# Trunk kernel: the conv mixer's weights in place from the first full period on, with four u buffers and five v buffers

## The reference, cut to what matters

```
a = rms_norm(x); z = a @ w_in                       # rwkv | conv | gates
o_r = rwkv7(z_rwkv) @ rwkv_w_o                      # 512 x 1024 weights ("w_r")
o_c = conformer_conv(z_conv) @ conv_w_o             # 512 x 1024 weights ("w_c")
h = x + (g_r * o_r + g_c * o_c) @ w_out
c = rms_norm(h)
# PEER: 8 heads x 16 = 128 experts per token, of 16384
idx, gates = top_k_product_keys(c @ w_q)
coef = gates * gelu(<c, u_tab[idx]>)                # one row of 4 KB per token and expert
h = h + sum_e coef_e * v_tab[idx_e]                 # another row of 4 KB
h = h + sigmoid(rms_norm(h) @ w_gate) * (p @ w_proj)
out = rms_norm(h)
```

## Time and profile before

| what | value |
|---|---|
| median of 3 runs | 3468.84 us (3466.03 to 3469.73) |
| the profiled execution | 3462.86 us, span 3461.2 us |
| DVE / PE / POOL busy | 69% / 78% / 57% of the span |
| data moved | 1253.76 MB, of it 1073.87 MB by the gathers (queue q0) |
| mean rate | 362 GB/s; 394 to 410 in the page's slices 11 to 35, which the full periods fill |

### The profile page before, as it was taken

How to read it: one execution, slowest core, us unless ns; L and a number is a source line. 1 busy time by engine, 2 the same in 40 slices (tenths; PEclk the granted TensorE clock), 3 DMA queues, 4 the chain that set the end, 5 groups by cost and what they waited for, 6 DMA issues and landing times.

```text
span 3461.2 us, 41395 instructions
## 1 busy us (share of the span) xinstructions
PE 2703.1 (78%) x15236; PEld 1218.4 (35%) x15236; DVE 2383.9 (69%) x6070; ACT 526.2 (15%) x1165; POOL 1970.5 (57%) x2093
## 2 busy tenths in 40 slices
PE   9987988898866777677677777786777678778887
PEld 7764655565423322332232323331333112111111
DVE  5549889988898779877987798779875677520000
ACT  3213212221211011101110021101110121110001
POOL 0003334333577676767676767666766667757663
PEclk9999999999889887988798968886888779789999
DMA  6547899889999999999999999999999999999995
GB/s 209 182 147 264 297 337 337 288 288 332 343 395 406 402 404 408 408 401 400 409 409 399 399 409 409 399 394 409 408 403 401 410 410 408 410 378 390 397 378 215
DMA packets 381194, 1253.76 MB, mean 362 GB/s; under 512 B 40384, under 2 KB 76480, under 8 KB 380224
## 3 DMA queue, kind: packets, MB, share of 16 engines
q0 software_dynamic: 294912, 1073.87, 79.9%
q1 hardware_dynamic: 83776, 176.20, 14.2%
q10 hardware_dynamic: 2304, 1.05, 0.1%
HBM read 1221.47 MB, written 29.49 MB: 361 GB/s over the span
## 4 chain that ended last, share of the span: by engine, by line
DMA 34%; PE 17%; POOL 14%; DVE 10%; issue 7%; ACT 0%; SPq 0%; POOLq 0%; ACTq 0%; DVEq 0%
DMA e_u<-in_u_tab,e_idx 14%; DMA e_v<-in_v_tab,e_idxT 10%; POOL e_v L780 7%; DMA e_a_rstd<-in_u_tab,e_idx 7%; PE e_acc L1087 5%; POOL e_u L763 5%; DVE e_u L1933 3%; PE e_acc L1157 3%; PE e_pd L985 3%; PE e_pd L1056 2%; POOL e_a_rstd L763 1%; DMA e_u<-in_v_tab,e_idxT 1%; DVE e_a_rstd L1933 1%; DMA e_x<-h_after_experts 1%; DVE e_gbc L1662 1%
## 5 line engine op out<-in xcount | busy, mean ns | idle before, releaser
L1087 PE MATMUL e_acc<-e_v,e_wd 128*32 128x512 f32 x3636 | 1112.8, 725 | 494.8 <-DMA e_v<-in_v_tab,e_idxT 480.2
L763 POOL DMA_INDIRECT e_u<-in_u_tab,e_idx x820 | 792.6, 967 | 903.0 <-DVE e_dots L1933 516.7
L1933 DVE CUSTOM_DVE_ANT_0 e_u<-e_u,e_c 128x1024 f32<-128x1024 f32 x820 | 996.2, 1215 | 378.9 <-DMA e_u<-in_u_tab,e_idx 373.4
L780 POOL DMA_INDIRECT e_v<-in_v_tab,e_idxT x909 | 863.6, 950 | 332.3 <-issue 218.6
L1087 PEld LDWEIGHTS e_acc<-e_v,e_wd 128*32 128x32 f32 x3636 | 147.7, 116 | 1141.3 <-DMA e_v<-in_v_tab,e_idxT 931.0
L1157 PE MATMUL e_acc<-e_v 128*128 128x384 f32 x1216 | 429.7, 499 | 11.6 <-ACT e_wd L1368 11.6
L1933 DVE CUSTOM_DVE_ANT_0 e_a_rstd<-e_a_rstd,e_c 128x1024 f32<-128x1024 f32 x204 | 247.8, 1215 | 94.7 <-DMA e_a_rstd<-in_u_tab,e_idx 94.1
L1662 DVE SCALAR_TENSOR_TENSOR e_gbc<-e_hc,e_cw,e_gbc 128x128 f32<-128x128 f32 x960 | 309.3, 343 | 1.2
L1157 PEld LDWEIGHTS e_acc<-e_v 128*128 128x128 f32 x1216 | 225.2, 193 | 160.4 <-issue 33.6
L763 POOL DMA_INDIRECT e_a_rstd<-in_u_tab,e_idx x204 | 196.6, 964 | 146.6 <-DVE e_dots L1933 115.4
L1942 DVE TENSOR_TENSOR e_hh<-e_hh,e_acc 64x512 f32<-64x512 f32 (+1 forms) x24 | 16.4, 682 | 249.6 <-PE e_acc L1087 249.1
(11 more groups left out here) (268 smaller groups left out, 2681.0 us busy)
## 6 DMA issues: line engine op xcount, KB each, us to landing
e_v<-in_w_in SPq DMA_DIRECT2D x76, 512.0 KB, 6.1
e_u<-in_w_in SPq DMA_DIRECT2D x38, 512.0 KB, 3.8
e_v<-in_v_tab,e_idxT POOLq DMA_INDIRECT x909
e_u<-in_u_tab,e_idx POOLq DMA_INDIRECT x820
e_ring<-in_w_c SPq DMA_DIRECT2D x32, 256.0 KB, 11.5
e_zb<-in_w_c SPq DMA_DIRECT2D x32, 256.0 KB, 8.4
e_ring<-in_w_r SPq DMA_DIRECT2D x32, 256.0 KB, 6.4
e_zb<-in_w_r SPq DMA_DIRECT2D x32, 256.0 KB, 9.0
```

Source lines behind the costliest of these rows:

```text
L763: pool.indirect_dma_start(out=u[m % UR][:, :], out_offset=None, in_=io["u_tab"], in_offset=bass.IndirectOffsetOnAxis(ap=idx[n % 2][:, j:j ...
L780: pool.indirect_dma_start(out=v[i], out_offset=None, in_=io["v_tab"], in_offset=bass.IndirectOffsetOnAxis(ap=idxT[n % (LAG + 1)][:, k:k + ...
L1087: last = pe.matmul(acc[rows, cols], w[:, at_:at_ + 32], v[v_place(m)[0]][:, cols], start=(step == 0), stop=True, skip_group_check=True)
L1933: dve.tensor_tensor_reduce(u[m % UR][:, :], u[m % UR][:, :], c[:, :], 1.0, 0.0, ALU.mult, ALU.add, dots[n % 2][:, j:j + 1]).then_inc(s_dot, 1)
```

## The change

From the front of tile 3 on, which runs in period 2 (`RESIDENT_FROM = 3`), the eight `w_c` blocks lie in eight fixed places and are not loaded again: the four `e_ring` buffers, the two halves of the sixth v buffer and the two halves of `e_a_rstd`. They are loaded once, in period 2. From period 2 on the u side therefore has four buffers (`u_place`, `u_user`; five in periods 0 and 1) and the v side five. The `w_r` blocks go through six places in `e_zb` (`stream_load`): blocks 0 to 5 when the recurrence is done, blocks 6 and 7 after the y products 0 and 1 have freed the first two places. In periods 8 and 9, where the mixer no longer runs, v again has eleven buffers.

```diff
-UR, UW, VR, RING, RINGS = 5, 4, 6, 4, 8
+UR, UW, VR, VW, RING, RINGS = 4, 4, 5, 6, 4, 8
+U_EARLY, RESIDENT_FROM, W_R = UR + 1, 3, 6
+VL = VR + UR + 2
+def u_place(m):
+    early = (RESIDENT_FROM - 1) * NSEL
+    if m < early:
+        return m % U_EARLY, m // U_EARLY + 1
+    i, k = (m - early) % UR, (m - early) // UR + 1
+    return i, len(range(i, early, U_EARLY)) + k
+def u_user(m):
+    early = (RESIDENT_FROM - 1) * NSEL
+    if m < early:
+        return m - U_EARLY if m >= U_EARLY else None
+    i = (m - early) % UR
+    return m - UR if m - early >= UR else range(i, early, U_EARLY)[-1]
...
+        v = [v_all[:, i, :] for i in range(VR)] + [u[i][:, :] for i in range(UR)] + [v_all[:, VR, :], a_rstd[:, :]]
+        w_c = [r[:, :, :] for r in ring[0:RING]] + [x[:, i * PAIRS * P:(i + 1) * PAIRS * P].rearrange("p (i t) -> p i t", i=PAIRS)
+                                              for x in (v_all[:, VR, :], a_rstd) for i in range(2)]
...
+            def resident_load(m):
+                first = RESIDENT_FROM
+                if m < RING:
+                    sp.wait_ge(s_wu, 2 * KT * (first - 1) + RINGS + m + 1)
+                elif m < RING + 2:
+                    sp.wait_ge(s_bm, BLOCKS * COL_TILES)
+                else:
+                    sp.wait_ge(s_dot, (first - 1) * NSEL)
+                sp.dma_start(w_c[m], io["w_c"][m]).then_inc(s_ring[RESIDENT_AT], 16)
+
+            def stream_load(n, m):
+                if m < W_R:
+                    sp.wait_ge(s_rp, REC_PE * 2 * (n + 1))
+                else:
+                    sp.wait_ge(s_wu, 2 * KT * n + KT + m - W_R + 1)
+                i = stream_turn(n, m)[0]
+                sp.dma_start(w_r[m % W_R][:, :, :], io["w_r"][m]).then_inc(s_ring[i], 16)
...
-                for k in ring_loads_at(n, s):
-                    ring_load(n, k // KT, k % KT)
+                if n < RESIDENT_FROM:
+                    for k in ring_loads_at(n, s):
+                        ring_load(n, k // KT, k % KT)
+                else:
+                    if n == RESIDENT_FROM and 40 <= s < 40 + KT:
+                        resident_load(s - 40)
+                    for m in range(KT):
+                        if s == (MIX_AT + m if m < W_R else product_slot(KT + m - W_R)):
+                            stream_load(n, m)
...
-                if m >= UR:
-                    pool.wait_ge(s_dot, m - UR + 1)
+                if u_user(m) is not None:
+                    pool.wait_ge(s_dot, u_user(m) + 1)
```

More of the change, by code:

```diff
@@ L177, in v_user @@
         return m - VR if m >= VR else None
-    if m - alone >= VR + UR:
-        return m - VR - UR
+    if m - alone >= VL:
+        return m - VL
     return m - VR if m - alone < VR else None
@@ L331, in trunk @@
         flat_zb = zb[:, :, :, :, :, :].rearrange("p c w i a t -> p (c w i a t)")
-        ring += [flat_zb[:, i * PAIRS * P:(i + 1) * PAIRS * P].rearrange("p (i t) -> p i t", i=PAIRS) for i in range(RINGS - RING)]
+        w_r = [flat_zb[:, i * PAIRS * P:(i + 1) * PAIRS * P].rearrange("p (i t) -> p i t", i=PAIRS) for i in range(W_R)]
+        ring += w_r[0:RINGS - RING]
         arena = buf("e_arena", [P, 34 * P])
@@ L360, in trunk @@
         pt = gbc[:, 0, 0:PLE // P, :]
-        u = [*(buf(f"e_u{i}", [P, D]) for i in range(UW)), a_rstd]
-        v_all = buf("e_v", [P, VR, D])
-        v = [v_all[:, i, :] for i in range(VR)] + [u[i][:, :] for i in range(UR)]
+        u = [buf(f"e_u{i}", [P, D]) for i in range(UR)]
+        u_all = [*u, a_rstd]
+        v_all = buf("e_v", [P, VW, D])
+        v = [v_all[:, i, :] for i in range(VR)] + [u[i][:, :] for i in range(UR)] + [v_all[:, VR, :], a_rstd[:, :]]
+        w_c = [r[:, :, :] for r in ring[0:RING]] + [x[:, i * PAIRS * P:(i + 1) * PAIRS * P].rearrange("p (i t) -> p i t", i=PAIRS)
+                                              for x in (v_all[:, VR, :], a_rstd) for i in range(2)]
         wd = [buf(f"e_wd{i}", [P, QUARTER * WROW]) for i in range(2)]
@@ L371, in trunk @@
         w_a = [u[i][:, :].rearrange("p (k c) -> p k c", k=KT) for i in range(UW)]
-        w_b = [v[3 + i].rearrange("p (k c) -> p k c", k=KT) for i in range(BW)]
+        w_b = [v_all[:, 3 + i, :].rearrange("p (k c) -> p k c", k=KT) for i in range(BW)]
         taken = blocks_at + KT * BEHIND_T
@@ L458, in trunk @@
         s_c = sem("e_tile_switched")
-        s_u = [sem(f"e_u_in{i}") for i in range(UR)]
-        s_v = [sem(f"e_v_in{i}") for i in range(VR + UR)]
+        s_u = [sem(f"e_u_in{i}") for i in range(U_EARLY)]
+        s_v = [sem(f"e_v_in{i}") for i in range(VL)]
         s_dot, s_gelu, s_coef = sem("e_dot"), sem("e_gelu"), sem("e_coef")
@@ L906, in mixer_product @@
             def mixer_product(n, which, m, x):
-                at_, turn = ring_turn(n, which * KT + m)
+                if n < RESIDENT_FROM:
+                    at_, turn = ring_turn(n, which * KT + m)
+                    w = ring[at_]
+                elif which:
+                    at_, turn = stream_turn(n, m)
+                    w = w_r[m % W_R]
+                else:
+                    at_, turn = RESIDENT_AT, 2 * RESIDENT_FROM + KT
+                    w = w_c[m]
                 pe.wait_ge(s_ring[at_], 16 * turn)
                 for i in range(PAIRS):
-                    last = pe.matmul(pd[:, m * P:(m + 1) * P], ring[at_][:, i, :], x[:, i, :],
+                    last = pe.matmul(pd[:, m * P:(m + 1) * P], w[:, i, :], x[:, i, :],
                                      start=(i == 0), stop=(i == PAIRS - 1))
@@ L1929, in dot @@
                 m = n * NSEL + j
-                dve.wait_ge(s_u[m % UR], 16 * (m // UR + 1))
+                i, turn = u_place(m)
+                dve.wait_ge(s_u[i], 16 * turn)
                 if j == 0 and n >= 2:
                     dve.wait_ge(s_gelu, n - 1)
-                dve.tensor_tensor_reduce(u[m % UR][:, :], u[m % UR][:, :], c[:, :], 1.0, 0.0, ALU.mult, ALU.add,
+                dve.tensor_tensor_reduce(u_all[i][:, :], u_all[i][:, :], c[:, :], 1.0, 0.0, ALU.mult, ALU.add,
                                          dots[n % 2][:, j:j + 1]).then_inc(s_dot, 1)
```

16 lines of the change are left out of this document (12 added, 4 removed).

## The result

| | before | after |
|---|---|---|
| median of 14 runs each | 3467.64 us (3461.78 to 3471.38) | 3478.78 us (3474.46 to 3485.37) |
| ratio, with its 95% interval | 1 | 1.0036 [1.0028, 1.0044] |
| the profiled execution | 3462.86 us, span 3461.2 | 3478.78 us, span 3477.1 |
| data moved | 1253.76 MB | 1245.37 MB |

The account below looks back on a forecast made before the run. The prediction took the full periods to be bound by DMA bytes. -20.5 us for bytes, +25.6 and +2.6 for buffers and 0 for moved loads gave +7.7 us, 3476.5 us at the runs' level, range 3447 to 3500.

Parts of the forecast that it names:

- Bytes, -20.5 us: Fronts of tiles 4 to 7: 32 `w_c` loads, 8.39 MB, go and save 20.5 us at 409 GB/s.
- its bound: Loads at a period's start: if their removal brought nothing, 10.3 us of the saving would be missing.
- Two dips per front, +2.56 each, and 2.6 for period 7: Behind slot 65's reciprocal and at the `w_out` products, five fronts: +25.6 us for the shorter queue; period 7 +2.6.
- the upper bound: Buffer losses 1.5 times as large, 42 us, if stalls the larger reserve covered, as at a period's start, show too.
- Quiet stretches at no cost: Undisturbed slots: four u buffers leave 8.75 us for transfer and queue, above 7.9, so 409 GB/s stays and cost is 0.
- The two other signs forecast for these stretches: Quiet stretches: 8 to 9 us from issue to dot, and POOL waiting for dots instead of "issue".
- The need: Time from a gather's issue to its dot that keeps the DMA engines full: between 6.0 and 7.9 us.
- the rival that the loop of four is a bound itself: u gathers: the four-buffer loop needs 10.3 us, 2.58 a slot against 2.56; 3492 to 3507 us; chance 0.16.
- u decides: Quiet stretches: the v loop has 12.8 us and a product shorter than a slot, so the u side sets the pace.
- Late `w_r` blocks at 0: Blocks 6 and 7, loaded after y products 0 and 1, land just in time: 0 us, bounds 0 and 17.5.
- Periods: Periods 3 to 6 stay at about 359 us; period 2 gets longer by 5.
- The rival that the queues don't need the buffers: At the dips the queue is not short for lack of a buffer: -20.5 us, 3448.3 us; chance 0.30.

Follow-up runs that it names:

- Buffers only: The changed kernel with all mixer weights still loaded for every tile, so only the two gather buffers go: 3491.20 us, 1.0070 against the kernel before.
- five v buffers alone: Five v buffers in place of six, five u buffers kept, all weights loaded as before: 3482.40 us, 1.0045 against the kernel before.
- four u buffers alone: Four u buffers in place of five from period 2 on, six v buffers kept, all loads as before: 3475.66 us, 1.0024 against the kernel before.
- first set: First runs of the kernels with both buffers, one u buffer, one v buffer or the bytes removed; the kernel before took 3666.72 us there.
- turned switch: The changed kernel with the rotation of four u buffers in period 2 beginning at `e_u1` in place of `e_u0`: 3477.62 us, 1.0033 against the kernel before.
- second and third set: Later runs, with repeats of the first kernels and new variants, where the kernel before took 3465.46 and 3466.26 us.

## Why the prediction held, and where it did not

**The whole.** The mechanism, bytes against the reserve of the queues, is what the runs show; the sign and the range were right. The time was forecast as +7.7 us and is +12.5 by the ratio [9.7, 15.3]. Two sizes were off and partly cancel: the bytes bring 11.8 us in the changed kernel where 20.5 were forecast, and the buffers cost 24.3 where 28.2 were.

**Bytes, -20.5 us.** Right where the buffers stay: -21.6. Not right in the changed kernel. Buffers only is at 1.0070 and the changed kernel at 1.0036, so with nine buffers the same 8.39 MB bring 0.0034 x 3467 = 11.8 us. +24.3 and -21.6 would make +2.7; about 10 us don't add, give or take 7 by the three intervals. The table shows the largest part in slots 8 to 23: with nine buffers, removing the `w_c` loads raises the idle there from 4.2 to 13.1 us, 8.9 of the 10.3 that these loads are worth; with eleven, from 0.0 to 3.3. The prediction had this as its bound ("if nothing came of those at a start, 4 x 2.56 = 10.3 us would be missing") and took the other end, because the saving of 2.56 us fitted into DVE's free 2.76. That was an argument on DVE's mean over 67 us. In slots 8 to 23 DVE has 39.42 of 39.91 us of work, so it can hardly run faster than the 40.58 us of before. The loads went out just ahead of this stretch (1655.25 us in the kernel before, 13.4 us to land), and what was left of them in the queue covered POOL's wait of 3 us at slot 8. Without them nine buffers leave the queue too short there, the rows at slot 8 show it, and the freed transfer time is idle; with eleven buffers the queue covers the wait by itself.

**Two dips per front, +2.56 each, and 2.6 for period 7.** Right in kind, wrong in size, and that 24.3 came near 28.2 is in part luck. With the buffers alone removed, the yardstick for periods 3 to 6 gives 3.0 and 7.0 us for the two dips where 4 x 2.56 = 10.2 was forecast for each. The start of a period adds 4.2, and periods 2 and 7 add 6.2 and 5.1 where 5.1 and 2.6 were forecast. Five v buffers alone lose 11.1 us in the four `w_out` stretches, 2.8 a front, which is the forecast size; four u buffers alone lose 2.4 behind the reciprocal, 0.6 a front. From before to after, periods 3 to 6, four fronts: slots 72 to 79 lose 3.2 us, 0.8 a front, and slots 88 to 103 6.8, 1.7 a front, where 2.56 was forecast for each. The loss at the start of a period, named only as the reason for the upper bound, is 13.1 us, 3.3 a front. My reading of the sizes, which no run tests by itself: where the queue ran dry before, one pair less in it costs only the part that no load of SP's queue fills; where the longer queue just covered the stall, all of the shortfall is new.

**Quiet stretches at no cost.** Right: 409 over 60 us. The two other signs forecast for these stretches were wrong, the 8 to 9 us from issue to dot and POOL waiting for dots. POOL, first and last of five u gathers in it, and the dot on the gather of 1747.76:

```profile
1747.76 0.94 POOL L824 DMA_INDIRECT e_u<-in_u_tab,e_idx  x1 [0.30 <-issue]
...
1757.92 0.93 POOL L824 DMA_INDIRECT e_u<-in_u_tab,e_idx  x1 [0.30 <-issue]
```

```profile
1754.79 1.22 DVE L2004 CUSTOM_DVE_ANT_0 e_u<-e_u,e_c 128x1024 f32<-128x1024 f32 x1 [0.46 <-DMA e_u<-in_u_tab,e_idx]
```

The dot starts 7.0 us after the gather (8 to 9 were forecast) and the next gather into its buffer goes out at 1757.92, long after the dot's end at 1756.01. POOL does not wait for dots here; four gathers in (1757.92 - 1747.76) / 4 = 2.54 us each are its own pace with one disturbed issue. The rate over the 12 us round it:

```profile
1744.00:1756.00 12.00, 7.86 (x104) 3.44 (x100) 9.67 (x21) 1.90 (x5) 9.23 (x10) 1.00 1.03 408
```

So 7.0 us from issue to data carry the plateau. The need was bounded between 6.0 and 7.9, although the prediction's own row of 405 GB/s at 7.6 us was against 7.9; it is at most 7.0, and the stretch at 350 GB/s with 7.9 us was short of something else; POOL waits for PE there, so probably of v rows. This also answers the rival that the loop of four is a bound itself: that took 10.3 us a turn, and here 7.0 and 1.5 us of a turn of 10.16 are used. Where DVE is full it had a point: at slot 8 a landed row waits for DVE, and POOL with it.

**u decides.** "Its product is shorter than a slot, so in quiet stretches u decides" had no part in the sum, since quiet stretches cost nothing in either case. What I made of it afterwards, that the u buffer is the dearer one, failed. In the `w_out` stretch PE is the late consumer, and there the v buffer counts; it is the dearer of the two, 15.6 us [10.7, 20.1] against 8.3 [5.2, 11.4].

**Late `w_r` blocks at 0.** Right. PE's waits for these blocks in the whole program, from the view of the mixer product's line, after the change:

```profile
  DMA e_zb<-in_w_r: 5.1, 4
```

and before:

```profile
  DMA e_zb<-in_w_r: 8.6, 8
```

All of these waits lie before period 2, where both kernels load the weights in the same way. The same view cut to the full periods lists none, in either kernel. So in the five fronts whose last blocks stand behind gates and `e_arena` in SP's list, PE never waited for them, as forecast; the blocks land in a median of 9.3 us (before 9.0).

**Periods.** Periods 3 to 6 last 1435.6 / 4 = 358.9 us (forecast about 359; before 358.1). Period 2 is longer by 2.8 us (361.14 to 363.98), half of the forecast 5; period 7 by 1.4 (342.64 to 344.02). These sum to 7.4 us. The profiled execution is 15.9 above that of before, since period 2 also begins 8.0 us later (928.38 to 936.42 for the first dot). POOL's wait at the switch is 1.9 us of that. The changed kernel, run again, begins period 2 at 941.52, so several us there differ from one run to the next, and the medians differ by 11.1 and not by 15.9.

**The rival that the queues don't need the buffers** is out: two buffers fewer cost 24.3 us with all loads as before. The Trainium skill's page "DMA: Bandwidth & Descriptors", section "Anatomy of one DMA — SWDGE (gpsimd) path", has a transfer as a fixed 2 us or so plus its bytes over the rate. Worked out from that, an estimate, nine buffers in flight would do. The runs disagree with the estimate: one u buffer of the eleven is worth 8.3 us and one v buffer 15.6. It counts the latency only, while the reserve is there for the moments in which the consumer is late.

**Left open.** Why the first set's transfers were slow; how the 10 us that don't add divide exactly (the yardstick gives 13.9 us for them, 5.6 at the period's start, 4.0 behind the reciprocal, 0.8 at `w_out`, 3.5 elsewhere, with about 2 us of rounding); and whether the turned switch is worth its 3.5 us. A few us may also lie outside the full periods. From the first to the third write of c (periods 0 and 1, in which no buffer is missing yet) the six profiles of kernels built from the changed one, in the second and third set and the result, take 659 to 665 us, and the four of kernels built from the one before 657 to 662. The means are 4 us apart, and no run tests whether this is more than chance. If it is more, each of the three buffer costs above holds these 4 us, and the two single ones would sum to 16 us against 20 for both.

## What to carry to other kernels

Where transfers bound a kernel, a buffer is a reserve against its consumer's longest busy run: look for the stretch in which the consumer is full, price the buffer there and not in a quiet stretch, and price each side by its own consumer. Saved bytes are worth their time only if something can be moved in their place; where the compute engine is full and the queue is short, they turn into idle transfer time. Free the place for resident data first from what isn't a gather buffer: half of the weights kept in the old ring, with all buffers left, was worth 16 us in this kernel, all of them with two buffers gone cost 12.

## What the runs showed of the hardware

- In the first set, on chip 6 by the record, the kernel before took 3667 us against 3465 to 3468 in all others (chips 0 and 14 in the second and third set), with the same kernel. There the gathers ran at 319 to 341 GB/s over 120 us, at DMA shares of 0.88 to 0.95, and a comparison of kernels gave other ratios (the u buffer 1.0188 against 1.0024, the bytes 1.0007 against 0.9938). The ratios taken where transfers were slower did not carry over.
- Two stretches of 20 us of five v only in that set, in slots which the result's profiles run near the plateau:

```profile
1400.00:1420.00 20.00, 12.89 (x148) 6.63 (x148) 16.10 (x52) 2.93 (x6) 11.61 (x14) 0.74 0.95 349
1480.00:1500.00 20.00, 11.50 (x150) 6.17 (x152) 11.97 (x41) 1.80 (x5) 12.22 (x13) 0.78 0.90 325
```

In the second, DVE works 12 of 20 us, PE 11.5 and POOL 12.2, and the DMA engines 0.90: no engine is full, and the rate is 325.
